# The opening of a two-layer diffusion backbone on one core: scale rows loaded first, shift columns by products of their own, no filling products ahead of the turn

## The chip, the core and the metric

The kernel runs on one core of one Trainium2 chip. TensorE (PE) multiplies matrices, VectorE (DVE) and ScalarE (ACT) work on rows of 128 partitions, GpSimd (POOL) does the same more slowly and issues some transfers, SyncE (SP) issues nearly all transfers from the chip's large memory (HBM). The engines run side by side and wait for each other through semaphores. An engine works through its own instructions in the order in which they are written, and SP does so too: a transfer that stands behind a wait in SP's list isn't issued before the wait is over. The metric is the time of one execution on the device in microseconds (us).

## What is computed

A layer, for 128 context tokens and 512 latent tokens with 1024 features each, conditioned by a vector each:

```python
def modulation(cond, w_ada, b_ada):
    m = jax.nn.silu(cond) @ w_ada + b_ada
    return jnp.split(m[:, None, :], N_MOD, axis=-1)
...
    shift1, scale1, gate1, shift2, scale2, gate2 = modulation(cond, w_ada_l, b_ada_l)
    h = rms_norm(x, g_mix) * (1 + scale1) + shift1
    mo, k, v = mixer(h, w_in_l, lambda_l, subln_l, conv_l, w_out_l, lam_init, k_ctx, v_ctx)
    x = x + gate1 * mo
    h = rms_norm(x, g_ffn) * (1 + scale2) + shift2
    x = x + gate2 * ffn(h)
```

`w_ada` is a matrix of 1024 x 6144 for each layer, six groups of 1024 columns: group 0 is the first shift, group 1 the first scale, group 2 the first gate. `mixer` begins with the product of `h` and `w_in` (3072 columns), which gives keys, queries, values and the three inputs of a short convolution. Two such layers follow one another, and everything below happens at the very start of the first one.

## The kernel before

All activations lie in SBUF as feature x token, in 8 slabs of 128 features (`KB = 8`). Every large product is made of three products of high and low parts: each weight chunk of 128 x 1024 (`raw`, six buffers, loaded by SP) is split into `w_hi` (ACT, line 1415) and `w_lo` (DVE, line 1996), three chunks deep (`SPLIT = 3`); the activations are split into `a_hi` (ACT, line 1456) and `a_lo` (DVE, line 2027). A block of the input projection is one chunk of `w_in`: 8 slabs x 3 products x 2 halves of the tokens = 48 matmuls of 128 x 320 (line 798). The blocks come in the order k0 to k3, q0 to q3, v0 to v3, then the convolution's (`IN_SEQ[0]`). The norm's factor is not in `a_hi`; it is applied when a block's sums are read from PSUM, with `ss` (kept by `keep_rstd`, ACT line 1438, from the spread of the norm, PE line 823). The shift enters as four more columns of `a_hi` behind the 640 tokens (`TA = T + 4`): the products with `a_hi` have 324 columns in the second half, and the last four are the shift's share of the output.

**The opening** (`ADA_FIRST`) gets the shift and the scale of layer 0. Each group of `w_ada` is loaded as two quads of 2 MB, `quad(layer, group, half)`, all by SP: the first into `ada_raw`, the next three into `ada_pro`. PE multiplies a quad with the conditions (`weigh_conditions`, line 864, 16 matmuls that the trace shows as 32 records). When a group's two quads are through, ACT copies the rows out of PSUM (`take_rows`, line 1478, tile `pT`), PE turns them into columns (`turn_rows`, line 888), and DVE adds the bias (`modulation`, line 2074, tile `mods`) and for a scale also makes `gains` (line 2082), which `a_hi` and `a_lo` need. Between them PE sums the squares (`norm_sums`, line 815) and spreads the norm's factor (line 823). `keep_busy` (line 881) puts products of a tile of ones in between, whose result nobody reads. Then `two_blocks` makes k0 and k1 together, slab by slab, so that PE can follow `a_lo` as its slabs come.

**The gate's rows** (group 2) are two further quads which stand between the blocks: `("ada", "rows", 2, 0)` behind k1, `("ada", "rows", 2, 1)` behind q1, and `("ada", "turn", 2, 0)` behind q2. Both quads are loaded into `ada_raw` by `load_rows`, and each load waits until PE is through with the quad before it:

```python
sp.wait_ge(mm_done, ROWS_AT[u - 1] + 1)
sp.dma_start(ada_raw[:], quad(l, grp, q)).then_inc(ada_full, 16)
```

SP issues the weight chunks of the projection in the same list. In it, `load_rows` for the second quad stands behind chunk 5 (q1), then come `lam_qk`, the cached keys and values (`load_cache`) and chunk 6 (q2).

**Who waits for whom between the blocks.** At the item of block c, ACT first splits chunk c + 2 (`split_hi`), then adds the bias to block c; DVE first makes the `w_lo` of chunk c + 2 (`split_lo`), then reads block c out of PSUM (lines 2044 to 2048), waits for ACT's bias, and turns keys and queries by their positions (lines 2230 to 2233). The DVE's part of the gate's rows is an item in the same list: a copy (line 2094) for the first quad, an addition (line 2096) for the second. Only after that addition is `row_done` raised, and PE's `turn_rows` for the gate waits for it.

Of the kernel before, what the change touches and what calls it, by code (L numbers as in the profile page):

```python
# [9 lines left out]
P = 128  # L10
D = 1024
KB = D // P
CTX, LAT, PAST = 128, 512, 256
T = CTX + LAT
# [116 lines left out]
for _e in range(EXPERTS):  # L131
# [5 lines left out]
ADA_FIRST = [("rows", 0, 0), ("norm", 0, 0), ("rows", 0, 1), ("spread", 0, 0), ("rows", 1, 0), ("turn", 0, 0),  # L137
             ("rows", 1, 1), ("turn", 1, 0)]
ADA_BLOCK = {("rows", 0): 1, ("rows", 1): 2, ("turn", 0): 3, ("turn", 1): 3, ("norm", 0): 4, ("spread", 0): 4}
# [10 lines left out]
KEEP_BUSY = {("rows", 0, 0): 40, ("norm", 0, 0): 4, ("rows", 0, 1): 2, ("spread", 0, 0): 0, ("rows", 1, 0): 8,  # L150
             ("turn", 0, 0): 0, ("rows", 1, 1): 2, ("turn", 1, 0): 2}
# [44 lines left out]
for _c, (_kind, _j) in enumerate(IN_KINDS):  # L196
    for _l in range(LAYERS):
        IN_SEQ[_l].append((_kind, _j))
        if _kind == "gc":
# [4 lines left out]
                   {("k", 1): ("ada", "rows", 2, 0), ("q", 1): ("ada", "rows", 2, 1), ("q", 2): ("ada", "turn", 2, 0)})  # L204
# [62 lines left out]
ROWS_AT = [AT[0, "ada"][1] + ADA_FIRST.index(("rows", 0, 0))] + [  # L267
    AT[_l, _stage][1] + _i for _l, _stage, _seq in ((0, "in", IN_SEQ[0]), (0, "ffn", DENSE))
    for _i, _item in enumerate(_seq) if _item[:2] == ("ada", "rows")]
ROWS_FIRST = [AT[0, "ada"][1] + ADA_FIRST.index(("rows", _g, _q)) for _g in range(2) for _q in range(2)]  # L270
# [12 lines left out]
def hybrid_step(nc, xT, condT, ada_w, in_w, out_w, gu_w, down_w, router_w, b_ada, g_mix, g_ffn, g_fin, lam_qk,  # L283
                subln, conv_w, kcT, vc, cos, sin, ident, iota, below, moe_down_w, y, newk, newv):
    with ExitStack() as ctx:
# [201 lines left out]
        ada_full = sem("ada_full")  # L487
        ada_in = [sem(f"ada_in{i}") for i in range(2)]
# [134 lines left out]
        def _(sp):  # L623
# [24 lines left out]
            sp.dma_start(ada_raw[:], quad(0, 0, 0)).then_inc(ada_full, 16)  # L648
            sp.dma_start(ada_pro[:, 0], quad(0, 0, 1)).then_inc(pro_full[0], 16)
            sp.dma_start(ada_pro[:, 1], quad(0, 1, 0)).then_inc(pro_full[1], 16)  # L650
            for hf in range(2):

                two = slice(2 * hf, 2 * (hf + 1))
                sp.dma_start(ada_pro[:, 2, two, :], quad(0, 1, 1)[:, two, :]).then_inc(pro_full[2 + hf], 16)
# [3 lines left out]
            for l in range(LAYERS):  # L658
                w = 0
                for item, c in IN_ITEMS[l][0]:  # L660
                    if c == 2 and l == 0:
                        for dst, src in late:
                            sp.dma_start(dst[:], src).then_inc(late_in, 16)
                    if c == RAW:
                        if l == 0:
                            sp.wait_ge(mm_done, ROWS_FIRST[-1] + 1)
# [116 lines left out]
        def _(pe):  # L783
# [122 lines left out]

            pe.wait_ge(ones_set, 1)
            for l in range(LAYERS):

                if l == 0:  # L910
                    n0, q0, g0 = AT[l, "ada"]
                    pe.wait_ge(cs_ready, 1)
                    for kind, grp, q in ADA_FIRST:
                        spread_done = (kind, grp, q) in ADA_FIRST[ADA_FIRST.index(("spread", 0, 0)) + 1:]
                        keep_busy(g0 + ADA_BLOCK["turn" if spread_done else "norm", 0], KEEP_BUSY[kind, grp, q])
                        g = g0 + ADA_BLOCK[kind, grp]
                        if (kind, grp, q) == ("rows", 0, 0):
                            pe.wait_ge(ada_full, 16)
                            weigh_conditions(ada_raw, g, q, True, False)
                        elif (kind, grp, q) == ("rows", 1, 1):  # L920
                            weigh_conditions(ada_pro[:, 2], g, q, False, True, pro_full[2:])
                        elif kind == "rows":
                            pe.wait_ge(pro_full[2 * grp + q - 1], 16)
                            weigh_conditions(ada_pro[:, 2 * grp + q - 1], g, q, q == 0, q == 1)
                        elif kind == "norm":
                            norm_sums(0)
                        elif kind == "spread":
                            norm_spread(0)
                        else:
                            pe.wait_ge(fold_ready, 1)  # L930
                            turn_rows(g, grp + 1, grp)
# [23 lines left out]
                two_blocks([(n0, g0), (n0 + 1, g0 + 1)], operand[l, "h1"], 2 * l if l else None)  # L955
# [1997 lines left out]
```

## Time and profile before

| | |
|---|---|
| median of 3 runs | 1850.8 us (1848.84 to 1851.08) |
| profiled execution | 1853.52 us, of which the span of the core is 1851.7 us |
| PE busy | 1788.8 us (97%) |
| DVE busy | 1267.1 us (68%) |
| ACT busy | 787.2 us (43%) |
| mean granted clock of TensorE | 0.988 |

Busy means that an instruction of the engine is under way; the share is of the span. The granted clock is the share of full speed at which TensorE was allowed to run: 1.00 is the level of 2.4 GHz, 0.50 the level of 1.2 GHz. Times in the trace count from the start of the span. The chain of waits follows the end of the kernel back to what released each piece of work; a piece shown there is one in which the end would have come earlier had it been shorter.

### The profile page before, as it was taken

The page shows a single profiled execution, that of the slowest core. Times are in us where ns is not written, and L with a number is a line of the kernel's source. Part 1 is how long each engine was busy: PE and PEld are TensorE (multiplying, and loading weights), DVE is VectorE, ACT ScalarE, POOL GpSimd, SP SyncE. Part 2 cuts the span into 40 slices and gives each one's busy share as a digit, 9 for nine tenths or more (in the row PEclk, how much of TensorE's full clock was granted, in tenths as well). Part 3 has the DMA queues.
Part 4 walks back from the last instruction along what each step waited for, and adds up shares of the span by engine and source line. Part 5 has one row for each costly group of instructions (what it writes and reads, how often), then busy time and mean ns, then how long its engine had stood idle before and what let it go on. Part 6 is the DMA issues. An engine that isn't in the chain of part 4 may idle for free.

```text
span 1851.7 us, 30287 instructions
## 1 busy us (share of the span) xinstructions
PE 1788.8 (97%) x11920; PEld 1666.8 (90%) x11920; DVE 1267.1 (68%) x2047; ACT 787.2 (43%) x1334; POOL 177.8 (10%) x180
## 2 busy tenths in 40 slices
PE   7998988999999999999999899899999999999997
PEld 6998956999999999999999669798989989899885
DVE  2677877557787767646735874475877778778787
ACT  4222255432221222223221563365656657566565
POOL 2000000110001000011000001232000000003221
PEclk8999999999999999999999999999999999999999
DMA  9445200234446444322222000296877778779862
GB/s 364 181 132 167 92 1 1 78 116 149 148 162 191 149 137 142 100 78 81 91 81 80 12 1 24 101 243 212 262 271 235 266 223 282 261 238 350 282 224 70
DMA packets 94707, 290.50 MB, mean 157 GB/s; under 512 B 16232, under 2 KB 24808, under 8 KB 94560
## 3 DMA queue, kind: packets, MB, share of 16 engines
q1 hardware_dynamic: 77280, 233.45, 38.3%
q0 software_dynamic: 17280, 55.05, 9.0%
q8 instruction: 97, 1.59, 0.3%
q14 instruction: 50, 0.41, 0.1%
HBM read 281.98 MB, written 12.28 MB: 159 GB/s over the span
## 4 chain that ended last, share of the span: by engine, by line
PE 86%; DVE 7%; ACT 2%; DMA 2%; issue 2%; SPq 0%; POOL 0%; POOLq 0%; DVEq 0%; ACTq 0%
PE ps L798 48%; PE ps L1177 11%; PE ps L1200 6%; PE ps L1178 5%; PE ps L1210 4%; PE ps L1005 2%; PE ps L948 2%; PE ps L1188 2%; PE ps L1181 2%; DVE nbias L2175 1%; DVE w_lo L1996 1%; DVE ada_raw L2116 1%; PE ps L1180 1%; DVE pr L2192 1%; PE ps L864 1%
## 5 line engine op out<-in xcount | busy, mean ns | idle before, releaser
L1996 DVE TENSOR_TENSOR w_lo<-raw,w_hi 128x1024 fp32r<-128x1024 f32 x394 | 481.7, 1224 | 299.4 <-ACT w_hi L1415 286.2
L1415 ACT ACTIVATE w_hi<-raw 128x1024 fp32r<-128x1024 f32 x394 | 414.1, 1053 | 296.2 <-PE ps L798 180.9
L1177 PE MATMUL ps<-hg,w_hi 128*128 128x320 f32 (+5 forms) x1232 | 345.3, 350 | 1.9 <-DVE w_lo L1996 1.3
L798 PE MATMUL ps<-a_hi,w_hi 128*128 128x320 f32 x1472 | 341.6, 313 | 3.4 <-DVE a_lo L2027 3.4
L798 PE MATMUL ps<-a_hi,w_lo 128*128 128x320 f32 x1472 | 337.2, 310 | 0.0
L798 PE MATMUL ps<-a_lo,w_hi 128*128 128x320 f32 x1472 | 334.5, 308 | 0.0
L1178 PE MATMUL ps<-hg,w_lo 128*128 128x160 f32 (+5 forms) x1232 | 300.1, 244 | 0.0
L798 PEld LDWEIGHTS ps<-a_hi,w_hi 128*128 128x128 f32 x1472 | 248.3, 189 | 9.0 <-issue 5.0
L798 PEld LDWEIGHTS ps<-a_lo,w_hi 128*128 128x128 f32 x1472 | 249.4, 189 | 0.0
L798 PEld LDWEIGHTS ps<-a_hi,w_lo 128*128 128x128 f32 x1472 | 245.8, 189 | 0.0
L1177 PEld LDWEIGHTS ps<-hg,w_hi 128*128 128x128 f32 x1232 | 232.0, 188 | 4.1 <-DVE w_lo L1996 2.3
L1178 PEld LDWEIGHTS ps<-hg,w_lo 128*128 128x128 f32 x1232 | 234.8, 191 | 0.4
L2116 DVE SCALAR_TENSOR_TENSOR ada_raw<-ada_raw,cs 128x1024 f32<-128x1024 f32 x126 | 155.9, 1279 | 2.3 <-DMA ada_raw<-ada_w 1.1
L1200 PE MATMUL ps<-w_hi,ea 128*128 128x512 f32 x308 | 85.6, 400 | 3.6 <-DVE w_lo L1996 3.6
L1949 POOL DMA_DIRECT2D ada_raw<-ada_w x72 | 38.3, 532 | 504.4 <-DVE ada_raw L2116 336.0
L798 PE MATMUL ps<-act_hi,w_hi 128*128 128x320 f32 x352 | 80.6, 310 | 0.0
L798 PE MATMUL ps<-act_lo,w_hi 128*128 128x320 f32 x352 | 80.1, 309 | 0.0
L798 PE MATMUL ps<-act_hi,w_lo 128*128 128x320 f32 x352 | 80.1, 309 | 0.0
L948 PE MATMUL ps<-kT,qT 64*128 64x512 f32 (+2 forms) x288 | 65.3, 501 | 12.0 <-ACT pr L1533 11.1
L1533 ACT ACTIVATE pr<-ps,nbias 128x768 f32<-128x768 f32 (+1 forms) x80 | 63.6, 795 | 27.1 <-DVE nbias L2175 15.8
L1626 ACT ACTIVATE act_hi<-tt 128x640 fp32r<-128x640 f32 x22 | 16.3, 741 | 137.9 <-DVE tt L2053 137.9
L2175 DVE TENSOR_REDUCE nbias<-ps 128x1 f32<-128x768 f32 (+1 forms) x80 | 62.8, 818 | 15.7 <-PE ps L948 14.9
(328 smaller groups left out, 2566.8 us busy)
## 6 DMA issues: line engine op xcount, KB each, us to landing
raw<-gu_w SPq DMA_DIRECT2D x220, 512.0 KB
raw<-moe_down_w SPq DMA_DIRECT2D x88, 512.0 KB
ada_raw<-ada_w POOLq DMA_DIRECT2D x72, 512.0 KB, 3.8
raw<-in_w SPq DMA_DIRECT2D x48, 512.0 KB
raw<-down_w SPq DMA_DIRECT2D x22, 512.0 KB
raw<-out_w SPq DMA_DIRECT2D x16, 512.0 KB
ada_raw<-ada_w SPq DMA_DIRECT2D x3, 2048.0 KB, 10.9
ada_pro<-ada_w SPq DMA_DIRECT2D x2, 2048.0 KB, 19.0
```

The source lines that it names most:

```text
L798: ins = nc.tensor.matmul(out[:, hf, 0:c1 - c0], w, o[:, c0:c1], start=f, stop=e)
L948: ins = nc.tensor.matmul(score_rows(l, m)[:, c0:c1], qT[rows, h, t * P:(t + 1) * P], kT[rows, h, k0 + c0:k0 + c1], start=True, stop=True)
L1177: nc.tensor.matmul(sums, whi, both, start=(k == 0), stop=False)
L1178: nc.tensor.matmul(out, wlo, rows_[:, k, 0, :], start=False, stop=False)
L1200: ins = nc.tensor.matmul(ps[:, g % 4, hf, :], ea[:, k, LOWER * a:LOWER * a + P], w[:, n % SPLIT, hf * 512:(hf + 1) * 512], start=(k == 0 a ...
L1210: ins = nc.tensor.matmul(ps[:, (g + 1) % 4, hf, :], ea[:, k, P:2 * P], w[:, n % SPLIT, hf * 512:(hf + 1) * 512], start=(k == 0 and w is w_ ...
L1415: nc.scalar.activation(w_hi[:, s, :], raw[:, n % RAW, :], ACT.Copy).then_inc(hi_done, 1)
L1533: nc.scalar.activation(pr[:, i % 2, s, 0:nk], score_rows(l, m)[:, 0:nk], ACT.Exp, bias=nbias[:, m % 4:m % 4 + 1], accum_out=rsum[:, STEPS[ ...
L1949: nc.gpsimd.dma_start(ada_raw[:, m % 2, :], ada_w[grp // 6, KB * (grp % 6) + k])\
L1996: nc.vector.tensor_tensor(w_lo[:, s, :], raw[:, n % RAW, :], w_hi[:, s, :].bitcast(F32), ALU.subtract)\
L2116: ins = nc.vector.scalar_tensor_tensor(ada_acc[:, c, :], part, share, ada_acc[:, c, :], op0=ALU.mult, op1=ALU.add)
L2175: nc.vector.tensor_reduce(nbias[:, m % 4:m % 4 + 1], score_rows(l, m)[:, 0:STEPS[m // 2][3]], AX, ALU.max, negate=True).then_inc(max_done, 1)
```

## The change

The scale's quads (group 1) are loaded and weighed first, the scale is turned at once, and k0 and k1 begin without the shift. The shift's two quads, the spread of the norm and the turn of the shift are put between the slabs of k0 and k1 (`ADA_BETWEEN`, in a new function `first_blocks`). The products of k0 and k1 have no shift columns any more; when the shift is there (`shift_ready`), 16 matmuls of four columns for each of the two blocks add its share. DVE now makes both halves of the shift columns. Of the filling products only the first 40 stay. Chunk 2 is split ahead of k0's item. The gate's first quad moves from behind k1 to behind k3.

```diff
+ADA_FIRST = [("rows", 1, 0), ("norm", 0, 0), ("rows", 1, 1), ("turn", 1, 0), ("spread", 0, 0), ("rows", 0, 0),
+             ("rows", 0, 1), ("turn", 0, 0)]
+ADA_OPENING = 4
+ADA_BETWEEN = {1: ADA_FIRST[4], 2: ADA_FIRST[5], 4: ADA_FIRST[6], 6: ADA_FIRST[7]}
...
+KEEP_BUSY = {("rows", 1, 0): 40, ("norm", 0, 0): 0, ("rows", 1, 1): 0}
...
-                   {("k", 1): ("ada", "rows", 2, 0), ("q", 1): ("ada", "rows", 2, 1), ("q", 2): ("ada", "turn", 2, 0)})
+                   {("k", 3): ("ada", "rows", 2, 0), ("q", 1): ("ada", "rows", 2, 1), ("q", 2): ("ada", "turn", 2, 0)})
...
+            def first_blocks(blocks, opnd):
...
+                for k in range(KB):
+                    pe.wait_ge(alo_done, opnd + k + 1)
+                    for n, g in blocks:
+                        if k == 0:
+                            pe.wait_ge(lo_done, n + 1)
+                            open_block(g)
+                        product(ps[:, g % 4], (n % SPLIT, k), a_hi[:, k, :], a_lo[:, k, :], k == 0, k == KB - 1)
+                    kind, _, q = ADA_BETWEEN.get(k, (None, 0, 0))
+                    if kind == "spread":
+                        norm_spread(0)
+                    g = AT[0, "ada"][2] + ADA_BLOCK["rows", 0]
+                    if kind == "rows":
+                        pe.wait_ge(pro_full[2 + q], 16)
+                        weigh_conditions(ada_pro[:, 1 + q], g, q, q == 0, q == 1)
+                    elif kind == "turn":
+                        turn_rows(g, 2, 1)
+                pe.wait_ge(shift_ready, 1)
+                for n, g in blocks:
+                    for k in range(KB):
+                        for w in (w_hi, w_lo):
+                            ins = nc.tensor.matmul(ps[:, g % 4, 1, HALF:HALF + TA - T],
+                                                   w[:, n % SPLIT, k * P:(k + 1) * P], a_hi[:, k, T:TA],
+                                                   start=k == 0 and w is w_hi, stop=k == KB - 1 and w is w_lo)
+                    ins.then_inc(mm_done, 1)
...
-                    act.wait_ge(mm_done, ROWS_FIRST[1] + 1)
-                    take_rows(0, g0)
-                    keep_rstd()
-                    act.wait_ge(mm_done, q0 + ADA_FIRST.index(("turn", 0, 0)) + 1)
-                    act.wait_ge(mm_done, ROWS_FIRST[3] + 1)
+                    act.wait_ge(mm_done, ROWS_FIRST[1, 1] + 1)
                     take_rows(1, g0)
                     split_hi(0, 0)
+                    gained(0, 0)
                     split_hi(1, 0)
-                    for kb in range(KB):
+                    for kb in range(1, KB):
                         gained(0, kb)
+                    keep_rstd()
+                    split_hi(2, 0)
+                    act.wait_ge(mm_done, q0 + ADA_FIRST.index(("turn", 1, 0)) + 1)
+                    act.wait_ge(mm_done, ROWS_FIRST[0, 1] + 1)
+                    take_rows(0, g0)
...
+                    split_lo(2)
+                    dve.wait_ge(row_done, 2)
+                    modulation(0, 0, g0 + ADA_BLOCK["turn", 0], q0 + ADA_FIRST.index(("turn", 0, 0)), 1)
+                    link(nc.vector.tensor_copy(a_hi[:, :, T:T + 2], mods[:, 0, 0:KB, :]))
+                    nc.vector.tensor_tensor(a_hi[:, :, T + 2:TA], mods[:, 0, 0:KB, :],
+                                            a_hi[:, :, T:T + 2].bitcast(F32), ALU.subtract).then_inc(shift_ready, 1)
+                    free_spread(0)
```

The first place is PE, from its first instruction to its first matmul of the projection. L881 (L884 after) are the filling products, L864 (L867) a quad's rows, L815 (L818) the sums of squares, L823 (L826) the spread, L888 (L891) a turn. Before:

```order
L881 MATMUL ps<-ones 128x128 x40
L864 MATMUL ps<-ada_raw,cs 32x256 x16
L881 MATMUL ps<-ones 128x128 x4
L815 MATMUL ps<-ones,ss 128x1 x5
L815 MATMUL ps<-ones,sq 128x1 x5
L881 MATMUL ps<-ones 128x128 x2
L864 MATMUL ps<-ada_pro,cs 32x256 x16
L823 MATMUL ps<-diag,ones 128x320 x2
L881 MATMUL ps<-ones 128x128 x8
...
L864 MATMUL ps<-ada_pro,cs 32x256 x16
L881 MATMUL ps<-ones 128x128 x2
L888 MATMUL ps<-fold,pT 128x8 x2
```

And after:

```order
L884 MATMUL ps<-ones 128x128 x40
L867 MATMUL ps<-ada_raw,cs 32x256 x16
L818 MATMUL ps<-ones,ss 128x1 x5
L818 MATMUL ps<-ones,sq 128x1 x5
L867 MATMUL ps<-ada_pro,cs 32x256 x16
L891 MATMUL ps<-fold,pT 128x8 x2
L801 MATMUL ps<-a_hi,w_hi 128x320 x2
```

Two quads, the spread, one turn and 16 filling products no longer stand ahead of the first matmul of the projection.

The second place is SP, from the first quad to the weight chunks behind the cache. `ada_raw` and `ada_pro` are quads or halves of one, `raw` are weight chunks. Before:

```order
L648 DMA ada_raw<-ada_w 128x4x1024
L649 DMA ada_pro<-ada_w 128x4x1024
L650 DMA ada_pro<-ada_w 128x4x1024
L654 DMA ada_pro<-ada_w 128x2x1024 x2
L629 DMA raw<-in_w 128x1024 x2
L641 DMA ada_raw<-ada_w 128x4x1024
...
L629 DMA raw<-in_w 128x1024 x4
L641 DMA ada_raw<-ada_w 128x4x1024
L667 DMA pr<-lam_qk 128x512
L632 DMA kT<-kcT 128x4x256
L633 DMA vtok<-vc 128x1024
L629 DMA raw<-in_w 128x1024 x18
```

And after:

```order
L654 DMA ada_pro<-ada_w 128x2x1024 x2
L631 DMA raw<-in_w 128x1024 x2
L662 DMA ada_pro<-ada_w 128x4x1024
L631 DMA raw<-in_w 128x1024
L664 DMA ada_pro<-ada_w 128x4x1024
...
L631 DMA raw<-in_w 128x1024
L643 DMA ada_raw<-ada_w 128x4x1024
L631 DMA raw<-in_w 128x1024 x2
L643 DMA ada_raw<-ada_w 128x4x1024
L670 DMA pr<-lam_qk 128x512
L634 DMA kT<-kcT 128x4x256
L635 DMA vtok<-vc 128x1024
```

The shift's quads moved behind chunks 1 and 2, and the gate's first quad behind chunk 3. The gate's second quad stands where it stood, with `lam_qk`, the cache and chunk 6 behind it, but its wait is for rows that PE now weighs two blocks later.

The third place is the end of k0 and k1 on PE, after the change (before, the quad L864 came here with nothing in between):

```order
L801 MATMUL ps<-a_hi,w_hi 128x320 x2
L801 MATMUL ps<-a_lo,w_hi 128x320 x2
L801 MATMUL ps<-a_hi,w_lo 128x320 x2
L933 MATMUL ps<-a_hi,w_hi 128x4
L933 MATMUL ps<-a_hi,w_lo 128x4
L933 MATMUL ps<-a_hi,w_hi 128x4
L933 MATMUL ps<-a_hi,w_lo 128x4
```

The pattern of L933 goes on for 32 matmuls in all.

## Rows read from the trace of the kernel before

**Rows 1.** The page's chain of waits, by engine

```profile
PE 86%; DVE 7%; ACT 2%; DMA 2%; issue 2%; SPq 0%; POOL 0%; POOLq 0%; DVEq 0%; ACTq 0%
```

**Rows 2.** Chain of waits in order of time: start us, us, what

```profile
17.59 2.89 PE ps L864 x32
...
22.23 2.13 PE ps L815 x20
...
24.91 3.23 PE ps L864 x32
28.14 1.55 PE ps L823 x4
...
40.88 16.58 PE ps L798 x96
57.47 1.86 PE ps L864 x32
...
96.77 0.34 PE ps L888 x4
97.12 14.19 PE ps L798 x96
```

**Rows 3.** Timeline of ACT and DVE: start us, us, engine, instruction, idle before

```profile
36.42 0.38 ACT L1478 ACTIVATE pT<-ps 128x256 f32<-128x256 f32 x1 [5.99 <-PE ps L864]
...
37.89 0.17 DVE L2082 SCALAR_TENSOR_TENSOR gains<-mods,gmix 128x16 f32<-128x16 f32 x1 [0.15 <-DVE mods L2074]
...
38.70 7.34 ACT L1456 ACTIVATE a_hi<-x,gains 128x128 fp32r<-128x128 f32 x16
...
39.82 1.01 DVE L2027 SCALAR_TENSOR_TENSOR a_lo<-x,gains,a_hi 128x128 fp32r<-128x128 f32 x2
```

**Rows 4.** Windows: stretch, us, busy us (instructions) by engine, clock, DMA share, GB/s

```profile
23.00:24.00 1.00, 1.00 (x12) 1.00 (x11) 0.00 (x0) 0.00 (x0) 0.00 (x0) 1.00 1.03 414
26.00:27.00 1.00, 1.00 (x13) 0.43 (x8) 0.00 (x0) 0.00 (x0) 0.00 (x0) 0.50 1.01 401
39.00:40.00 1.00, 0.00 (x0) 0.00 (x0) 0.47 (x3) 1.00 (x4) 0.00 (x0) 0.50 1.10 326
44.00:45.00 1.00, 1.00 (x5) 1.00 (x5) 1.00 (x4) 1.00 (x3) 0.00 (x0) 0.50 1.02 418
46.00:47.00 1.00, 1.00 (x9) 1.00 (x9) 1.00 (x3) 0.98 (x2) 0.00 (x0) 1.00 0.90 369
```

**Rows 5.** Timeline of SP: start us, us of the issue, transfer

```profile
7.09 0.53 SPq L649 DMA_DIRECT2D ada_pro<-ada_w  x1
...
59.39 0.38 SPq L641 DMA_DIRECT2D ada_raw<-ada_w  x1
...
61.08 0.69 SPq L633 DMA_DIRECT2D vtok<-vc  x1
```

**Rows 6.** DMA issues: transfer, how many, size, us from issue to landing

```profile
ada_pro<-ada_w SPq DMA_DIRECT2D x1, 2048.0 KB, 16.7
...
vtok<-vc SPq DMA_DIRECT2D x1, 512.0 KB, 11.7
```

**Rows 7.** Timeline of ACT (first row) and DVE between the blocks

```profile
77.40 1.04 ACT L1415 ACTIVATE w_hi<-raw 128x1024 fp32r<-128x1024 f32 x1
...
81.65 0.15 DVE L2046 TENSOR_REDUCE bcol<-ps 128x2 f32<-128x4 f32 x1
...
87.93 0.15 DVE L2046 TENSOR_REDUCE bcol<-ps 128x2 f32<-128x4 f32 x1
...
93.07 0.42 DVE L2096 TENSOR_TENSOR pT<-pT,ps 128x256 f32<-128x256 f32 x1
93.77 1.23 DVE L1996 TENSOR_TENSOR w_lo<-raw,w_hi 128x1024 fp32r<-128x1024 f32 x1 [0.27 <-DVEq L2098]
```

**Rows 8.** Timeline of PE in the routing stage: matmuls of few columns

```profile
1172.92 0.21 PE L1117 MATMUL ps<-mods,wr 128*8 128x2 f32 x8
...
1176.53 1.25 PE L1141 MATMUL ps<-four_sum,lgT 128*128 128x8 f32 x10
```

More of the change, by code:

```diff
@@ L132 @@
     LO_BASE.append(LO_BASE[-1] + 2 + FB + (2 * ST if _e == LAST_E else 0))
-ADA_FIRST = [("rows", 0, 0), ("norm", 0, 0), ("rows", 0, 1), ("spread", 0, 0), ("rows", 1, 0), ("turn", 0, 0),
-             ("rows", 1, 1), ("turn", 1, 0)]
-ADA_BLOCK = {("rows", 0): 1, ("rows", 1): 2, ("turn", 0): 3, ("turn", 1): 3, ("norm", 0): 4, ("spread", 0): 4}
+ADA_FIRST = [("rows", 1, 0), ("norm", 0, 0), ("rows", 1, 1), ("turn", 1, 0), ("spread", 0, 0), ("rows", 0, 0),
+             ("rows", 0, 1), ("turn", 0, 0)]
+ADA_OPENING = 4
+ADA_BETWEEN = {1: ADA_FIRST[4], 2: ADA_FIRST[5], 4: ADA_FIRST[6], 6: ADA_FIRST[7]}
+ADA_BLOCK = {("rows", 1): 1, ("turn", 1): 2, ("rows", 0): 3, ("turn", 0): 3, ("norm", 0): 4, ("spread", 0): 4}
 QUAD = 4
@@ L487, in hybrid_step @@
         ada_full = sem("ada_full")
+        shift_ready = sem("shift_ready")
         ada_in = [sem(f"ada_in{i}") for i in range(2)]
@@ L661, in _ @@
                     if c == 2 and l == 0:
+                        sp.dma_start(ada_pro[:, 1], quad(0, 0, 0)).then_inc(pro_full[2], 16)
+                    if c == 3 and l == 0:
+                        sp.dma_start(ada_pro[:, 2], quad(0, 0, 1)).then_inc(pro_full[3], 16)
                         for dst, src in late:
@@ L665, in _ @@
                         if l == 0:
[L666 removed]
+                            sp.wait_ge(mm_done, ROWS_FIRST[0, 1] + 1)
                             sp.dma_start(lq, lam_qk.partition_broadcast(P)).then_inc(lam_in, 16)
@@ L912, in _ @@
                     pe.wait_ge(cs_ready, 1)
-                    for kind, grp, q in ADA_FIRST:
-                        spread_done = (kind, grp, q) in ADA_FIRST[ADA_FIRST.index(("spread", 0, 0)) + 1:]
-                        keep_busy(g0 + ADA_BLOCK["turn" if spread_done else "norm", 0], KEEP_BUSY[kind, grp, q])
+                    for kind, grp, q in ADA_FIRST[:ADA_OPENING]:
                         g = g0 + ADA_BLOCK[kind, grp]
-                        if (kind, grp, q) == ("rows", 0, 0):
-                            pe.wait_ge(ada_full, 16)
[L919 to L928, printed above, removed]
-                        else:
-                            pe.wait_ge(fold_ready, 1)
-                            turn_rows(g, grp + 1, grp)
+                        if kind == "turn":
+                            pe.wait_ge(fold_ready, 1)
+                            turn_rows(g, 1)
+                            continue
+                        keep_busy(g0 + ADA_BLOCK["norm", 0], KEEP_BUSY[kind, grp, q])
+                        if kind == "norm":
+                            norm_sums(0)
+                        elif q == 0:
+                            pe.wait_ge(ada_full, 16)
+                            weigh_conditions(ada_raw, g, 0, True, False)
+                        else:
+                            weigh_conditions(ada_pro[:, 0], g, 1, False, True, pro_full[0:2])
                     u = 1
@@ L954, in _ @@
                 in_blocks = g0 + len(IN_SEQ[l])
-                two_blocks([(n0, g0), (n0 + 1, g0 + 1)], operand[l, "h1"], 2 * l if l else None)
+                if l == 0:
+                    first_blocks([(n0, g0), (n0 + 1, g0 + 1)], operand[l, "h1"])
+                else:
+                    two_blocks([(n0, g0), (n0 + 1, g0 + 1)], operand[l, "h1"], 2 * l)
                 for b, (item, c) in enumerate(IN_ITEMS[l][0]):
@@ L1451, in gained @@
                     act.wait_ge(mod_ready, i + 1)
+                if kb == 0 and i:
                     nc.scalar.activation(a_hi[:, :, T:T + 2], mods[:, l, 3 * which * KB:(3 * which + 1) * KB, :], ACT.Copy)
@@ L1506, in _ @@
                     kind, j = item[0], item[1]
-                    if c is not None:
+                    if c is not None and (l or c):
                         split_hi(n0 + c + 2, q0 + b)
@@ L2209, in _ @@
                         continue
-                    split_lo(n0 + c + 2)
-                    if b == 0:
+                    if l or c:
+                        split_lo(n0 + c + 2)
+                    if b == 0 and l:
                         free_spread(2 * l)
```

22 lines of the change are left out of this document (7 added, 15 removed).

## The prediction, made before the changed kernel ran

> **What bounds the kernel now.** I read the page's chain of waits first: PE holds 86% of it [rows 1], so a microsecond counts where PE waits, or where PE does work that could be elsewhere. The chain in order of time then shows the opening [rows 2]. PE weighs the first quad at 17.59, sums the squares at 22.23, weighs the second quad from 24.91 to 28.14, and only at 40.88 does the first matmul of the projection run. From there PE has no gap on the chain: k0 and k1 take 16.58 us, the gate's first quad 1.86, the gate's turn starts at 96.77, and q3 and v0 (96 matmuls, 14.19 us, so 7.1 a block) end at 111.31. What lies between the last quad's rows and the first product is in the timeline [rows 3]: ACT takes the rows out at 36.42, `gains` is there at 38.06, a slab of `a_hi` costs 0.92 (7.34 over 8), a slab of `a_lo` 1.01, ready at 40.83. The windows show the clock [rows 4]: 1.00 at 23 to 24, 0.50 at 26 to 27 after the narrow products of the norm's sums, 0.50 at 39 to 40, where PE stands from its turn, which is over before `gains` begins at 37.89 [rows 3], until 40.88, some 3 us, still 0.50 at 44 to 45 and 1.00 at 46 to 47. The price of a cold start can be read there: 96 matmuls took 16.58 us from the idle start and 14.19 us in q3 and v0, so 2.4 us.
>
> Last, SP's list [rows 5]. It waits until PE is through with the gate's first quad and issues the second at 59.39; `lam_qk`, the cache and chunk 6 stand behind it. The cached values, issued at 61.08, need 11.7 us [rows 6] and land at 72.8. Chunk 6 is next. ACT splits it at 77.40 [rows 7], so it came in time: the slack is at most 4.6 us, and about 3.4 if the chunk's 0.5 MB at some 410 GB/s [rows 4] add 1.3 us to the values' landing.
>
> **The opening: gained.** The first quad lands as before, its rows end at 17.59 + 2.89 = 20.48. Without the filling products the sums follow at once: 20.48 + 2.13 = 22.6. The scale's second quad lands at 7.09 + 16.7 = 23.8 [rows 5, 6], now in two halves of which the first is earlier; its rows take 3.23 at the low clock [rows 2] and the second half is needed at 22.6 + 1.6 = 24.2, so they end at 25.85. (At the high clock a quad takes 1.86; then the landing decides, and the end is about 24.8. I take the low clock, since nothing but the narrow sums runs ahead of it, as before the window at 26 to 27.) From the rows' end ACT starts 0.1 later, and `gains` is ready 38.06 - 36.42 = 1.64 after that: 27.6. Then one slab of `a_hi`, 0.92, while DVE makes the first `w_lo` (1.23 [rows 7]); `a_lo` starts at about 28.8 and ends 1.0 later. The first product runs at 29.75, which is 11.1 us earlier than 40.88. The second block's `w_lo` follows at about 31.0, and the first block's slab 0 lasts at the low clock until 31.4, so nothing waits. Chunks 0 and 1 stand directly behind the scale's quads: 23.8 + 2 x 1.3 is early enough for `w_hi`.
>
> **What PE gets between the slabs: lost again.** The spread took 1.55 at the low clock [rows 2]; between 0.8 (half of it) and 1.55 I take 1.1, since slab 1 ends about where the clock has come back. Two quads at 1.86: 3.7. A turn: 0.34. The 32 narrow products have no row of their own, four columns against whole 128 x 128 weights. Ten matmuls of eight columns with full weights took 1.25 us [rows 8], which is 0.11 to 0.125 each; eight of two columns with weights of only eight columns took 0.21, 0.03 each. So 32 cost between 0.8 and 4.0; I take 0.112 each, 3.6, since the weights are full. The weights then cost more than the columns. The Trainium skill ("TensorE: Matmul & The Clock Gate", "Back-to-back issue gap") gives matmuls of 1 to 64 columns a floor of about 25 ns, an estimate of 0.8 us for 32, and under "LDWEIGHTS (loading the stationary operand)" a load of 128 columns at 128/1.2 = 107 ns, an estimate of 3.4; the row with full weights sides with the second, and by the first the sum below would be 2.8 us smaller.
>
> The shift's quads come behind chunk 1 and chunk 2. At the rate of [rows 4] (2 MB in 5.1 us) they land at about 31.5 and 37.8; PE wants them after slab 2 and slab 4, at about 38.5 and 44. Hidden by 6 us or more; a late one would cost its lateness. DVE's four steps from the turn to `shift_ready` (each 0.17 to 0.3, about 1.0 together) lie beside slab 7, 12 matmuls at 0.148, 1.8 us: 0.7 us of cover. The columns that the blocks lose are nothing. So k0 and k1 end at 29.75 + 16.6 + 1.1 + 3.7 + 0.3 + 3.6 = 55.1 against 57.47: 2.4 us gained.
>
> **The gate's quads: a wait that is new.** Call the end of k1 E. Before, SP could issue the second quad at E + 1.9. Now PE goes through k2 and k3 first (2 x 7.1) and then through the first quad, so SP's wait ends at E + 16.1. Nothing that stands behind it in SP's list comes sooner: `lam_qk`, the cache and, above all, chunk 6. The cached values landed 72.8 - 59.39 = 13.4 after that issue, the chunk by my estimate at 14.65, so now at E + 30.75. The quad itself is ahead of them and in time.
>
> Who waits. ACT splits chunk 6 ahead of q0's bias, so it stands from about E + 18 on; DVE has the `w_lo` of chunk 6 ahead of reading q0, so it stands too. With 1.04 for `w_hi` and 1.15 for `w_lo`, DVE reads q0 at E + 33.05, q1 6.28 later [rows 7] (81.65 to 87.93), and comes to the addition of the gate's rows 5.14 after that (87.93 to 93.07): E + 44.5. The addition and its semaphore take 0.65, and PE may turn the gate's rows at E + 45.1. In the kernel before it did at 96.77, which is E + 39.3. q2 itself loses less than 1 us, waiting for its `w_lo` at E + 33.1 where it could begin at E + 32.1; it ends at E + 40.2. **The stall at the turn is 5.8 us in all.** Its bounds: with the chunk's landing no later than the values' (13.4) it is 4.6; with the landing as late as ACT's split allows (77.40 - 59.39 = 18.0) it is 9.2.
>
> **The clock after it.** PE stands for about 4.9 us, longer than in the opening, where the 3 us without work ended at 0.50 [rows 4]. q3 starts cold: up to the 2.4 us worked out above; I take 2.2. Behind it nothing gives this back: v0 ends PE-bound, DVE has its next `w_lo` ready about 0.3 us before, and the chain goes on from v0's end as it does now.
>
> **The sum.** -11.1 + 1.1 + 3.7 + 0.3 + 3.6 = -2.4; +5.8; +2.2: 5.6 us slower. The profiled execution took 1853.5 (span 1851.7) and would take 1859.1; it lies 2.7 above the median of the runs shown, 1850.8, and I give the time on the latter's scale: 1856.4. About 0.2% (3.7 us) is what a measurement of this kernel can tell from no change, so slower is beyond 1854.5.
>
> **The rivals.**
> - **The stall stays small or the clock holds**, 1852 to 1854.5: for it, the opening may gain 1.0 more (high clock at the second quad), a landing at 13.4 takes 1.2 off, and a clock that rises early takes 1.5 off. Against it, all must go one way. 0.16.
> - **The narrow products cool the clock**, 1858.0: the sums of squares, narrow too, ran at 1.00 and the window behind them had 0.50 [rows 4]. 3.6 us of narrow products might do the same to k2: some 1.6 us at half speed more. Against it, the quads and slabs around them are dense. 0.16.
> - **The narrow products cost nearly nothing**, 1853.6: they would stream as those with weights of eight columns, 0.8 instead of 3.6. Here this is the page's 25 ns floor as a mechanism. The trace speaks against it. 0.05, beside the first.
> - **The chunk comes in time: faster than before**, 1848.4 or less: if ACT and DVE had chunk 6 by 14.65 - 5.8 = 8.9 us after SP's issue, the turn would not wait and only the -2.4 would be left; with cheap narrow products too, -5.2. From a landing of 8.9 on it decides. The values alone landed at 13.4 with the same transfers ahead, so this needs another order of landing than SP's. 0.07.
> - **The forecast** as summed, 1854.5 to 1857.5: 0.56.
>
> **How the numbers follow.** The likeliest is 1856.4. The low end reaches into the first rival, 1852.8; the high end takes the cooled clock (1858.0) and part of the later landing: 1859.3. Left out are most of the faster case and the worst landings. Slower by over 0.2%: the forecast, the cooled clock and a little of the rest, 0.73. Within 0.2%: the small stall, the cheap products and half of the last rival, whose plain -2.4 is less than 3.7 us, 0.22. Faster: the rest of it, with cheap products or a warm opening on top, 0.05.
>
> **What would show it.** First matmul of the projection near 29.8 (a miss by 1 is the clock at the second quad). k1's end near 55, with the 32 narrow products starting about 0.11 apart. SP issuing the gate's second quad near 71, ACT's seventh `w_hi` near 86 with its wait put down to a transfer, a PE gap of nearly 5 us ahead of the gate's turn near 100, the granted clock at 0.50 behind it, and v0's end near 117 against 111.31. The prediction is wrong if ACT's seventh split isn't late, if PE goes from q2 to q3 without a gap, or if the lead gained or lost at v0 changes later.

## The result, and the profile after

The changed kernel takes 1862.93 us, the median of 6 runs (1859.54 to 1866.17), against 1850.94 for the kernel before in 6 runs of its own (1848.84 to 1855.45): a ratio of 1.0057 [1.0044, 1.0069]. It is slower, as forecast, but by about 10.5 us (0.57%) where 5.6 were forecast, and the time lies above the range of 1852.8 to 1859.3. The two medians are 12.0 us apart; this text goes by the ratio, since 71 later runs of the kernel before, in three groups, had medians of 1852.1 to 1852.9, and 1862.93 less 10.5 is 1852.4. The profiled execution took 1859.54 us, with a span of 1857.7.

The opening and the end of k0 and k1 are in the timeline of PE of the changed kernel (start us, us, instruction, how many, idle before). They answer to the opening in [rows 2].

```profile
17.34 1.93 PE L867 MATMUL ps<-ada_raw,cs 128*32 128x256 f32 x32 [2.57 <-DMA ada_raw<-ada_w]
19.20 1.28 PE L818 MATMUL ps<-ones,ss 128*128 128x1 f32 x10
...
23.96 1.93 PE L867 MATMUL ps<-ada_pro,cs 128*32 128x256 f32 x16 [1.15 <-DMA ada_pro<-ada_w]
...
30.17 0.90 PE L801 MATMUL ps<-a_hi,w_hi 128*128 128x320 f32 x2 [2.69 <-DVE a_lo L2059]
...
52.61 0.25 PE L933 MATMUL ps<-a_hi,w_lo 128*128 128x4 f32 x1
52.72 0.25 PE L933 MATMUL ps<-a_hi,w_hi 128*128 128x4 f32 x1
...
56.07 0.62 PE L801 MATMUL ps<-a_hi,w_hi 128*128 128x320 f32 x2
```

The first product of the projection is at 30.17, 10.7 us earlier than before. The narrow products start 0.11 us apart, one behind another for 3.5 us, and k2 starts at 56.07 where the quad behind k1 started at 57.47 before. Of 10.7 us gained, 1.4 are left.

The windows of the same kernel (as [rows 4]) show the granted clock at four places:

```profile
23.00:24.00 1.00, 0.04 (x4) 0.04 (x6) 0.00 (x0) 0.00 (x0) 0.00 (x0) 0.50 1.01 414
...
54.00:55.00 1.00, 1.00 (x11) 1.00 (x10) 0.47 (x2) 0.00 (x0) 0.00 (x0) 1.00 0.00 0
57.00:58.00 1.00, 1.00 (x5) 1.00 (x5) 0.95 (x2) 0.43 (x1) 0.00 (x0) 0.50 0.00 0
...
103.00:104.00 1.00, 1.00 (x5) 1.00 (x5) 0.97 (x4) 0.00 (x0) 0.00 (x0) 0.50 0.00 0
```

So there are three cold stretches: one that has begun by the quad's wait at 23 and lasts until about 36, one behind the narrow products at 57 although PE has had no gap, and one behind the gate's turn at 103.

What PE, ACT and DVE waited for between 60 and 110 us is in the view of waits (who and line, for whom: us in total, times, longest):

```profile
ACT w_hi L1444 <- DMA raw<-in_w: 12.8, 1, 12.8
...
PEld ps L891 <- DVEq L2132: 4.9, 1, 4.9
```

Each of these waits is there once. The timeline of SP, and behind it those of ACT and of DVE, say where:

```profile
73.85 0.38 SPq L643 DMA_DIRECT2D ada_raw<-ada_w  x1
```

```profile
87.56 1.06 ACT L1444 ACTIVATE w_hi<-raw 128x1024 fp32r<-128x1024 f32 x1 [12.84 <-DMA raw<-in_w]
```

```profile
89.79 0.16 DVE L2078 TENSOR_REDUCE bcol<-ps 128x2 f32<-128x4 f32 x1
...
101.19 0.42 DVE L2128 TENSOR_TENSOR pT<-pT,ps 128x256 f32<-128x256 f32 x1
```

SP comes to the gate's second quad at 73.85 (before 59.39 [rows 5]); the seventh chunk, whose split was at 77.40 before [rows 7], is split at 87.56; DVE reads q0 at 89.79 and comes to the addition of the gate's rows at 101.19, where it stood at 93.07 before [rows 7]. The chain in order of time begins, between 0 and 125 us, with what the addition lets go:

```profile
101.85 1.02 PE ps L891 x4
102.88 16.40 PE ps L801 x96
...
119.30 0.16 DVE bcol L2076
```

The turn takes 1.02 instead of 0.34 and the two blocks 16.40 instead of 14.19 [rows 2]: the turn and the start of the blocks run at the low clock. DVE reads v0 at 119.30, against 111.33: 8.0 us later.

### The profile page after: what moved, and what is told of

The parts are those of the page before. It is cut to its first block, busy times and chain, and to the rows that moved or that the text cites. A ratio compares the mean times of both kernels' runs of the same rounds, so it can differ in the third digit from the quotient of the medians.

```text
span 1857.7 us, 30277 instructions
## 1 busy us (share of the span) xinstructions
PE 1790.4 (96%) x11916; PEld 1668.9 (90%) x11916; DVE 1267.7 (68%) x2048; ACT 787.8 (42%) x1333; POOL 178.3 (10%) x180
## 4 chain that ended last, share of the span: by engine, by line
PE 81%; DVE 8%; ACT 2%; DMA 2%; issue 1%; POOL 0%; POOLq 0%; DVEq 0%; ACTq 0%; SPq 0%
PE ps L801 45%; PE ps L1206 11%; PE ps L1229 5%; PE ps L1207 5%; PE ps L1239 3%; PE ps L1034 2%; PE ps L974 2%; PE ps L1217 2%; PE ps L1210 2%; DVE w_lo L2028 1%; DMA raw<-gu_w 1%; DVE nbias L2209 1%; DVE ada_raw L2148 1%; PE ps L1209 1%; DVE pr L2226 1%
## 5 line engine op out<-in xcount | busy, mean ns | idle before, releaser
L1658 ACT ACTIVATE act_hi<-tt 128x640 fp32r<-128x640 f32 x22 | 16.3, 741 | 138.0 <-DVE tt L2085 138.0
L2209 DVE TENSOR_REDUCE nbias<-ps 128x1 f32<-128x768 f32 (+1 forms) x80 | 62.8, 818 | 16.1 <-PE ps L974 15.4
```

Source lines behind the costliest of these rows:

```text
L2209: nc.vector.tensor_reduce(nbias[:, m % 4:m % 4 + 1], score_rows(l, m)[:, 0:STEPS[m // 2][3]], AX, ALU.max, negate=True).then_inc(max_done, 1)
```

## The experiments

Each was timed against the kernel before on the same chip. "Edit of the changed kernel" below means that all the rest of the change is in it. Three columns of the table are read from one trace each: the first product of the projection, the end of k0 and k1, and DVE's first read of v0. The last but one is the start of ACT's 121st split of a weight chunk (997.5 in the kernel before) less that of before; it shows what the opening and layer 0 have done in all. A trace is of one execution and the ratio is of all runs: the traces of the changed kernel and of experiment 3 are of the fastest execution of their six, those of experiments 10 and 11 of the slowest of their ten and twelve.

| kernel | first product | end of k1 | v0 read | 121st split | ratio [interval] |
|---|---|---|---|---|---|
| before (three traces) | 40.67 to 41.41 | 57.40 to 57.47 | 111.27 to 111.33 | -0.1 to 0 | |
| changed | 30.17 | 56.07 | 119.30 | +7.6 | 1.0057 [1.0044, 1.0069] |
| 1 changed, again | 33.06 | 58.77 | 123.03 | +11.2 | 1.0054 [1.0041, 1.0067] |
| 2 other order on SP | 32.12 | 57.94 | 114.19 | +0.2 | 0.9998 [0.9989, 1.0006] |
| 3 before, gate's quad behind k3 | 40.71 | about 56.4 | 117.78 | +4.9 | 1.0041 [1.0028, 1.0055] |
| 4 changed, gate's quad behind k1 | 33.23 | 59.13 | 115.33 | +1.4 | 0.9992 [0.9984, 1.0001] |
| 5 fills ahead of the gate's turn | 30.01 | 55.69 | 118.10 | +6.4 | 1.0036 [1.0023, 1.0049] |
| 6 as 2, 4 narrow products | 32.68 | 54.38 | 108.35 | -3.4 | 0.9971 [0.9959, 0.9982] |
| 7 as 2, narrow ones mixed in | 32.00 | 56.06 | 110.08 | -3.1 | 0.9981 [0.9971, 0.9991] |
| 8 as 7, with fills | 30.12 | 53.11 | 106.96 | -7.2 | 0.9973 [0.9962, 0.9984] |
| 9 before, 40 fills only | 39.49 | 56.20 | 110.06 | -1.3 | 0.9988 [0.9978, 0.9998] |
| 10 before, again | 40.67 | 57.46 | 111.33 | -0.1 | 1.0001 [0.9991, 1.001] |
| 11 as 2, with fills | 34.33 | 59.05 | 115.20 | +1.3 | 0.9995 [0.9987, 1.0004] |

The end of k1 of experiment 3 is worked out: its quad starts at 70.63, and k2 and k3 ahead of it take 14.27, the figure that the next 96 matmuls in full clock take in the traces of experiments 2 and 6.

**1. The changed kernel once more.**

> The changed kernel once more, unedited. In its first trace v0's end came 8.0 us later than before (119.3 against 111.3) but the span grew by only 6.0, while the medians differ by about 11. Theory A (the late chunk 6): the opening and the turn repeat, chunk 6 near 87 and v0's end near 118 to 120; what the span adds or loses beyond 8 us comes from stretches at the low clock in the routing and expert stages, and differs from execution to execution. Rival B (something in layer 0 or 1 got slower for good): another stretch shows a constant extra shift in this trace too. Ratio expected 1.004 to 1.007.

The time repeats: 1862.86 us. The trace doesn't: DVE was expected to read v0 near 118 to 120 and does so at 123.03. The timeline of PE of this execution:

```profile
17.62 3.64 PE L867 MATMUL ps<-ada_raw,cs 128*32 128x256 f32 x32 [4.21 <-DMA ada_raw<-ada_w]
21.19 2.29 PE L818 MATMUL ps<-ones,ss 128*128 128x1 f32 x10
...
25.55 3.64 PE L867 MATMUL ps<-ada_pro,cs 128*32 128x256 f32 x32
...
33.06 0.90 PE L801 MATMUL ps<-a_hi,w_hi 128*128 128x320 f32 x2 [2.69 <-DVE a_lo L2059]
...
57.28 0.35 PE L933 MATMUL ps<-a_hi,w_lo 128*128 128x4 f32 x1
57.49 0.35 PE L933 MATMUL ps<-a_hi,w_hi 128*128 128x4 f32 x1
```

A quad takes 3.64 instead of 1.93 and the sums 4.4 instead of 2.3, since the clock has fallen while PE stood for 4.21 us ahead of the first quad (the 40 filling steps ahead of it were over sooner, in 10.53 us against 11.90). The first product comes 2.9 us later than in the first trace, and the last eight narrow products start 0.21 us apart instead of 0.11. k1 ends at 58.77, later than in the kernel before, and DVE reads v0 11.7 us later than before. The first trace had caught an opening in which the clock fell late. Seven traces have the same instructions up to the first product of the projection (the first one, 1, 2, 4, 5, 6 and 7): it lies at 30.01 to 33.23, in five of them at 32.00 or later, 31.9 in the mean.

**2. SP's order.** Edit of the changed kernel: SP issues `lam_qk`, the cache and chunks 6 to 8 ahead of the gate's second quad.

```diff
-                    if item[:3] == ("ada", "rows", 2):
+                    if item == ("ada", "rows", 2, 1):
+                        pass
+                    elif item[:3] == ("ada", "rows", 2):
                         load_rows(u, 0, 2, item[3])
...
                         n, w = n + 1, w + 1
+                        if l == 0 and c == 8:
+                            load_rows(u, 0, 2, 1)
+                            u += 1
```

> The changed kernel, but SP issues lam_qk, the cache and chunks 6 to 8 ahead of the gate's second quad, so that none of them stands behind its wait. PE, ACT and DVE keep their order. Theory A: chunk 6 is there in time, the gap ahead of the gate's turn and the cold stretch behind it are gone, and v0's end comes 8 to 9 us earlier than in the changed kernel, near 110.5; ratio to the kernel before 0.998 to 1.001. Rival C (the loss is in the opening: narrow products, cooled clock, inserted work): v0's end stays near 119 and the ratio above 1.004.

1852.17 us, 0.9998 of before. The timeline of SP, and then the chain in order of time:

```profile
76.33 0.38 SPq L643 DMA_DIRECT2D ada_raw<-ada_w  x1
```

```profile
53.61 4.33 PE ps L938 x32
57.94 16.46 PE ps L806 x96
...
92.40 7.23 PE ps L806 x48
99.63 0.34 PE ps L896 x4
99.97 14.19 PE ps L806 x96
```

SP still waits until 76 for the quad (76.33, behind the cache and three chunks), but nothing that anyone needs stands behind that wait. PE has no gap ahead of the turn, the turn takes 0.34, and q3 and v0 take 14.19. All that the gate's quad cost is gone. What is left of the change's own loss is in the first two pieces: 4.33 for the narrow products, and 16.46 for k2 and k3 at a clock that was low from 56 to about 62.8. For these two DVE reads v0 at 114.19 and not near 110.5, as was expected.

**3. The gate's quad alone.** Edit of the kernel before: the gate's first quad behind k3, nothing else.

```diff
-                   {("k", 1): ("ada", "rows", 2, 0), ("q", 1): ("ada", "rows", 2, 1), ("q", 2): ("ada", "turn", 2, 0)})
+                   {("k", 3): ("ada", "rows", 2, 0), ("q", 1): ("ada", "rows", 2, 1), ("q", 2): ("ada", "turn", 2, 0)})
```

> The kernel before with one part of the change alone: the gate's first quad behind k3 instead of k1. Theory A: SP's wait ends near 73.5 instead of 59.4, chunk 6 lands near 88.5, the gate's turn runs some 5.8 us late with a cold clock behind it, v0's end near 119 to 120 against 111.3, 7 to 9 us slower, ratio 1.004 to 1.005. Rival C: the quad is hidden wherever it stands, no more than 1 us, ratio 1.000.

1860.09 us, 1.0041 of before: most of the loss, from one key of a table. Its waits, its SP and its chain (three views of this kernel) are those of the changed kernel:

```profile
ACT w_hi L1415 <- DMA raw<-in_w: 10.2, 1, 10.2
...
PEld ps L888 <- DVEq L2100: 4.9, 1, 4.9
```

```profile
72.63 0.38 SPq L641 DMA_DIRECT2D ada_raw<-ada_w  x1
```

```profile
100.53 1.02 PE ps L888 x4
101.56 16.20 PE ps L798 x96
```

**4. The other way round.** Edit of the changed kernel: the same key, back to `("k", 1)`.

> The changed kernel with the gate's first quad back behind k1. That also puts its load ahead of the shift's two quads in SP's list, so these land about 5 us later (near 36 and 44), just when PE wants them. Theory A: no gap ahead of the gate's turn, at most 2 us of waiting for the shift's quads; v0's end 110 to 112, ratio 0.998 to 1.002. Rival C: v0's end stays above 117.

1850.93 us, 0.9992 of before. The chain in order of time:

```profile
54.79 4.34 PE ps L933 x32
59.13 3.57 PE ps L867 x32
...
100.77 0.34 PE ps L891 x4
101.11 14.19 PE ps L801 x96
```

No gap at the turn here either. The quad that now stands behind the narrow products takes 3.57 instead of the 1.86 of [rows 2]: the clock is low behind them, with a quad there as with a block. DVE reads v0 at 115.33 where 110 to 112 was expected, by the cold opening (first product at 33.23) and this stretch. The edits of experiments 2 and 4 have nothing in common but that the chunk is in time, and both take 1.0054 to no change.

**5. Filling products ahead of the gate's turn**, to keep the clock through the stall. Edit of the changed kernel:

```diff
                         if item[1] == "turn":
+                            if item[2] == 2:
+                                open_block(g0 + b)
+                                keep_busy(g0 + b, 14)
                             turn_rows(g0 + b, item[2] + 1)
```

> The changed kernel with 14 filling products (some 4.1 us at full clock) ahead of PE's wait for the gate's turn; they go to the turn's own PSUM buffer and nobody reads them. Theory A: the gap of 4.9 us is filled, the turn still starts near 102 to 105, but the clock stays at 1.00, so q3 and v0 take 14.2 us instead of 16.4: 2.2 us off the changed kernel, ratio to the kernel before about 1.0042. Rival D (the cold stretch behind the turn is not due to PE's standing): the clock falls all the same and nothing changes.

1858.8 us, 1.0036. The 28 filling matmuls took 3.29 us from 96.95, and the last 1.5 us ahead of the turn stayed empty. The windows:

```profile
102.00:103.00 1.00, 1.00 (x9) 1.00 (x9) 1.00 (x2) 0.00 (x0) 0.00 (x0) 1.00 0.00 0
...
105.00:106.00 1.00, 1.00 (x5) 1.00 (x5) 0.89 (x3) 0.98 (x2) 0.00 (x0) 0.50 0.59 225
```

The turn and the first products run at 1.00, but the clock still falls, from about 103.1 to 106.5, so the two blocks take 15.74 instead of 16.40. The test is half a success: it bears out that the cold clock is a part of the loss, and it doesn't give the whole price, because the clock wasn't held. Its interval and that of the changed kernel overlap at their ends.

**6. Four narrow products instead of 32.** Edit of experiment 2: `for k in range(1)` in the loop of the narrow products, so that the shift's share of seven of the eight slabs is left out of k0 and k1.

> The SP order of e2, with 2 narrow products a block instead of 16: the shift's share of slabs 1 to 7 in k0 and k1 is left out, so those keys are not the reference's. Theory A with the cooled clock: 28 products at 0.112 (3.1 us), their second part at the low clock (0.7) and the cold stretch behind them (1.7 to 3.3) go: 5 to 6.5 us off e2, ratio to the kernel before 0.9965 to 0.9975. Rival E (the narrow products cost their own time and the clock falls anyway): only 3.1 to 3.8 us, ratio near 0.998.

1847.35 us, 0.9971. The chain:

```profile
54.05 0.34 PE ps L938 x4
54.38 14.18 PE ps L806 x96
```

Four take 0.34, and k2 and k3 take 14.18 where experiment 2 had 16.46. 28 narrow products less give 4.0 us of their own and 2.3 us of clock behind them.

**7. The same products, mixed with wide ones.** Edit of experiment 2: the two quads come behind slabs 2 and 3 and the turn behind slab 4; for slabs 6 and 7, which come last, the products carry their own shift columns, and the 24 narrow products of slabs 0 to 5 stand between them, two ahead of each pair of wide ones.

```diff
+            def narrow(n, g, k):
+                for w in (w_hi, w_lo):
+                    nc.tensor.matmul(ps[:, g % 4, 1, HALF:HALF + TA - T], w[:, n % SPLIT, k * P:(k + 1) * P],
+                                     a_hi[:, k, T:TA], start=False, stop=False)
...
+                        for kk in range(3 * (k - 6), 3 * (k - 5)):
+                            narrow(n, g, kk)
+                            ins = part(n, g, k, kk - 3 * (k - 6))
```

> The SP order of e2, with the narrow products of slabs 0 to 5 put between the wide products of slabs 6 and 7, which carry their own shift columns again; the shift's second quad is weighed behind slab 3 and turned behind slab 4. 24 narrow products instead of 32, no stretch of narrow products alone. If the clock falls because narrow products stand alone: it stays at 1.00 through k2, and 2.5 to 4 us go off e2, ratio 0.9975 to 0.9985. If narrow products cool it wherever they stand: about 1 us off, ratio 0.999.

1848.83 us, 0.9981: with everything computed, and faster than before. The timeline of PE:

```profile
55.05 0.25 PE L918 MATMUL ps<-a_hi,w_lo 128*128 128x4 f32 x1
55.16 0.54 PE L926 MATMUL ps<-a_lo,w_hi 128*128 128x320 f32 x2
...
55.68 0.54 PE L926 MATMUL ps<-a_hi,w_lo 128*128 128x320 f32 x2
56.06 0.46 PE L806 MATMUL ps<-a_hi,w_hi 128*128 128x320 f32 x2
```

A group of two narrow and two wide ones takes 0.52, of which the wide ones alone would take 0.29: a narrow one still costs 0.11. What mixing changes is the clock. The window from 57 to 58 has 1.00 here and 0.50 in experiment 2. The number went down from 32 to 24 with the mixing; no run has 24 in a row or 32 mixed, so how much each of the two does isn't shown.

**8. And the opening kept warm.** Edit of experiment 7: 49 filling steps instead of 40 at the start, 4 ahead of the scale's second quad, 7 behind the scale's turn.

```diff
-KEEP_BUSY = {("rows", 1, 0): 40, ("norm", 0, 0): 0, ("rows", 1, 1): 0}
+KEEP_BUSY = {("rows", 1, 0): 49, ("norm", 0, 0): 0, ("rows", 1, 1): 4}
...
                             turn_rows(g, 1)
+                            keep_busy(g0 + ADA_BLOCK["norm", 0], 7)
```

> e7 with filling products again: 49 instead of 40 at the start, 4 ahead of the scale's second quad, 7 behind the scale's turn, to keep the clock at 1.00 until the first product of the projection. If that works: first product near 29, slabs 0 and 1 at full clock, 2 to 3 us off e7, ratio 0.996 to 0.9975. If the clock is low there anyway, the fills cost double and it is e7 or up to 1.5 us slower.

1846.58 us, 0.9973 [0.9962, 0.9984]: faster than both kernels. The chain:

```profile
17.50 1.93 PE ps L872 x32
19.44 2.32 PE ps L823 x20
...
23.20 3.09 PE ps L872 x32
...
30.12 1.15 PE ps L806 x6
31.28 2.96 PE ps L806 x18
```

The first quad and the sums run at the high clock, the second quad doesn't; the first product starts at 30.12 with the clock at 1.00, and 24 matmuls take 4.1 where they took 5.3 in experiment 2. The gain over experiment 7, 0.0008, is smaller than either interval, though the 121st split is 4.1 us earlier in the trace.

**9 to 12. What the old filling products were worth, and the kernel before again.** Edit of the kernel before: all entries of `KEEP_BUSY` at 0 but the first, 40 (experiment 9). Experiments 10 and 12 are the kernel before unedited, and experiment 11 is experiment 2 with the `KEEP_BUSY` lines of experiment 8.

> The kernel before with the filling products alone taken out: only the first 40 stay, as in the change. In that kernel the quads' landings set the pace (the last at 34.4), so the 1.8, 0.7, 2.0, 0.7 and 0.7 us of fills lie in waits. Theory F (the fills' absence is part of the loss): the clock is low when the last quad is weighed and the rows and turns take twice as long on the path, first product up to 2 us later, ratio up to 1.001. Rival G (they are neutral here): ratio 0.9995 to 1.0005.

> The kernel before once more, unedited, for a second trace to hold the others against. If v0's end in the first trace (111.4) was typical, it is within 1 us of that here. If the opening of the first trace was a lucky one, it is 112 to 115. Ratio 1.000.

> e2 (narrow products alone at the end of k1) with the fills of e8. Tells the fills from the mixing in e8. If the fills give what e8 was ahead of e7 (0.8 in 1000): ratio about 0.999 against 0.9998 in e2, with the cold stretch behind the narrow products still there. If the fills only help with the mixing: 0.9998.

> A third trace of the kernel before: v0's end between 111 and 115, as in e10's expectation.

Experiment 9: 1850.56 us, 0.9988 [0.9978, 0.9998], with v0 read 1.3 us earlier. It was expected to lose, or to change nothing. Its chain begins the last stretch of the opening with a transfer and not with work of PE:

```profile
13.80 19.94 DMA ada_pro<-ada_w
...
39.49 16.71 PE ps L798 x96
```

In the kernel before, the filling products of the opening, meant to hold the clock, end up in the way of quads that have landed. Experiment 10: 1852.72, 1.0001 [0.9991, 1.001]; experiment 12: 1851.69 in one run. In three traces the kernel before has v0 read within 0.1 us, although its first product moved by 0.7 us (40.67, 40.88, 41.41): k0 and k1 behind it took 16.79, 16.58 and 15.99, the less the later they began, since less of them ran at the low clock. Experiment 11: 1850.37, 0.9995. Its first quad landed 1 us later than in experiment 8, the sums ran cold again (4.36), and k1 ended at 59.05, so in that trace, of the slowest of its twelve executions, the fills alone bought nothing; over all runs, 0.9995 and the 0.9998 of experiment 2 can't be told apart.

## Why the prediction was right in kind and too small in size

**Right: the stall and its mechanism.** SP's wait, the late chunk, ACT, DVE and the turn came in the order that was written, and experiments 2, 3 and 4 show it from three sides: with the quad moved alone the loss is there, with the quad moved back or the wait taken from in front of the chunk it is not. The terms, counted from k1's end: in the first trace after the change, SP issues at 73.85 - 56.07 = +17.8 (forecast +16.1), the turn starts at +45.8 (forecast +45.1). Experiment 3 has them without a cooled k2: +16.3 and +44.2, so a stall of 44.2 - 39.3 = 4.9 us against 5.8. The step that was too long is the chunk's landing, 14.65 behind SP's issue; ACT splits it 13.6 behind it there (86.24 - 72.63).

**Right: the cold clock behind it,** 2.2 forecast. Measured: 0.68 for the turn, which was not in the sum, and 2.0 to 2.4 for the two blocks, 2.7 to 3.1 in all.

**Right: the price of a narrow product,** 0.112 us while the clock is high. All of them have full weights, like the row of [rows 8] from which the price was taken, and cost far more than the 0.8 us for 32 of the rival with cheap products. No run changes the size of their weights.

**Wrong: "-11.1 + 1.1 + 3.7 + 0.3 + 3.6 = -2.4".** The opening gave 1.4 us in one trace and lost 1.3 in the other; k1's end in the traces of the same opening with the 32 narrow products (the first, 1, 2, 4 and 5) is 56.07, 58.77, 57.94, 59.13 and 55.69, a mean of 57.5, so nothing was gained. From the first product to k1's end these five take 25.7 to 25.9 us against 25.3 in the sum; the larger part is the -11.1, the first product at 29.75 where the mean of seven traces is 31.9. The step that failed is "its rows end at 17.59 + 2.89 = 20.48 [...] 20.48 + 2.13 = 22.6": the first quad and the sums with the durations of one trace of the kernel before. The sums took 4.36 us in five of the seven traces (1, 2, 4, 6 and 7), 2.3 and 2.5 in the other two. In the kernel before, filling products stood between quad and sums, and the clock was back at 1.00 when the sums ran (window from 22 to 23, in the trace behind [rows 4]); in experiments 2, 6 and 7 the sums come straight behind the quad, and the windows from 20 to 26 all have 0.50. The first quad took 1.93 to 3.64 instead of 2.89. That isn't the work of the change, since the 40 filling steps ahead of it stayed: in three traces of the kernel before it took 2.44, 2.89 and 3.59. The working weighed the clock for the second quad and for slab 0 and not for these two terms. When the clock falls in the opening stays open: experiment 9 has no filling products between quad and sums either, and its sums ran at 1.00.

**Wrong: the chance of the cooled clock.** It was a rival with 0.16 at 1858.0. It happened in every trace with the 32 narrow products in a row behind k1: windows at 57 with 0.50 (0.58 in experiment 4). "The quads and slabs around them are dense" was the argument against, and it doesn't count: PE was recorded busy throughout. It costs 1.7 us in the first trace (73.85 was to be 72.2) and up to 2.3 in k2 and k3 (16.46 against 14.18), and 0.7 more where the last narrow products themselves run cold (4.33 against 3.6). The sums of squares in [rows 4] had pointed to it, and experiments 6 and 7 show it by taking it away.

**The sum again.** For the first trace: -1.4 for k1's end, +6.5 from there to the turn (4.8 of stall and 1.7 of cooled k2), +2.9 for turn and blocks: 8.0, as read. The second trace: +1.3, +7.3, +3.1: 11.7. The 10.0 and 10.5 of the runs lie between. Against the forecast of 5.6 that is about 2.4 for the opening, the cold narrow products among it, 2 for the cooled k2, 0.7 for the turn, less 1.0 for the landing: 9.7 in all, so 0.8 of the measured 10.5 isn't accounted for. Another 1.6 us of the distance from 1856.4 to 1862.93 are the scale: 1850.8 was the median of three runs, and the later runs of the kernel before lie near 1852.4.

**What changes behind v0.** The prediction would be wrong if the lead at v0 changed later, and it does, by 1.8 to 2.8 us in experiments 2, 4, 7, 8 and 11 (from the read of v0 to the 121st split), by 1.5 in experiment 3, and hardly in the changed kernel (8.0 to 7.6). The windows of the kernel before and then of experiment 7 show the place of the larger part:

```profile
150.00:160.00 10.00, 7.67 (x43) 6.29 (x44) 6.85 (x10) 2.07 (x3) 1.14 (x3) 0.66 0.51 162
```

```profile
150.00:160.00 10.00, 9.26 (x62) 8.53 (x63) 5.26 (x9) 1.96 (x3) 1.06 (x2) 0.83 0.57 199
```

A mean of 0.66 over 10 us is 6.8 us at 0.50, and one of 0.83 is 3.4 us: at the same wait of PE near 150 us the clock is low half as long, and from 230 to 240 the mean is 0.84 and 1.00. Nothing was tried on it: why the same wait costs more clock in one kernel than in another stays open, and so does why three executions of the kernel before, within 0.1 us of each other at the 121st split, end 6.0 us apart (spans of 1849.8, 1851.7 and 1855.8). These are as large as the differences of experiments 7 and 8 from each other and from the kernel before, so which part of their gain is the opening and which is such a difference can't be said from the medians alone; the traces put 1.3 and 4.4 us at v0.

## What to carry to other kernels

When an item moves on which an in-order queue waits, list all that stands behind that wait in the queue and ask who needs it and when; here an item that no one missed made a 12.8 us wait for one that three engines needed, and putting the wait behind the needed transfers was worth as much as undoing the move. Work that is moved earlier on PE is worth only what the clock lets it be worth: take no duration over from a stretch whose filling the change removes, and none from one trace where the clock moves. Many matmuls of a few columns with full weights are best put between wide ones, where in experiment 7 they cost their 0.11 us each and nothing behind them.

## What the runs showed of the hardware that was not expected

- The granted clock falls to 0.50 while and behind a run of narrow matmuls in which PE is recorded as busy the whole time: the window at 54 has 1.00 and PE busy 1.00, the one at 57 has 0.50 and PE busy 1.00. Mixed with wide matmuls, 24 of them leave it at 1.00.
- A narrow matmul with full weights takes 0.11 us at the high clock and 0.21 at the low one, so it follows the clock like a wide one; a quad takes 1.93 and 3.64.
- In the opening of the changed kernel the same instructions bring the first product at any time from 30.0 to 33.2 us. In the first trace the clock holds through the first quad and the sums (1.93 and 2.3 us, behind a wait of 2.57), in experiment 1 it is low for both (3.64 and 4.4, behind a wait of 4.21), and in experiment 5 it is low for the quad and back for the sums (3.41 and 2.5, behind a wait of 3.22). The kernel before moves by 0.7 us in three traces, and its v0 by 0.1.
- In the kernel before, the filling products behind the first 40 cost 1.3 us up to v0 in the trace of experiment 9 (the runs: 0.9988, an interval that ends at 0.9998): its quads had landed, and PE was what they waited for.
